# Stick-breaking attention, two heads at a time: values in column halves, products on POOL, copies shared

## Chip, core and metric

The kernel runs on one core of one Trainium2 chip. The metric is the device time of one execution in microseconds (us). Its engines are PE (matmul; PEld is its weight load), ACT, DVE and POOL; SP issues the DMAs. PSUM has 8 banks of 512 fp32 columns on 128 partitions.

## What is computed

A decoder layer on 1024 tokens of width 1024: SwiGLU, a mixer, cross attention into 256 memory tokens, SwiGLU, norm. The change lies in the mixer's stick-breaking attention, 8 heads of 64:

```python
z = jnp.einsum("bhqd,bhkd->bhqk", q_blk, k_pre) * scale      # 128 queries, keys up to them
strict = k_pos[None, :] < q_pos[:, None]
log_rest = jnp.where(strict, jax.nn.log_sigmoid(-z), 0.0)
suffix = lax.cumsum(log_rest, axis=3, reverse=True) - log_rest
a = jnp.where(strict, jnp.exp(jax.nn.log_sigmoid(z) + suffix), 0.0)
outs.append(jnp.einsum("bhqk,bhkd->bhqd", a, v_pre))
```

A weight is thus sigmoid(z) of its key times the product of sigmoid(-z) over all later keys.

## The kernel before

All engines run programs written out by hand, in order, with semaphores. Most of the span is three-pass matmuls of split operands (`three`, L917 to L919). The stick-breaking stage is one loop over `M` = 64 tiles; tile m is head m//8 and a block i of 128 queries, against 128(i+1) keys, so its rows are 128 to 1024 wide. `PAIR_ORDER` takes the blocks of a head as 0,1, 6,7, 2,3, 4,5. At step s:

- PE (L1240): `scores(s)` (L1203 low keys, L1206 the mask on the diagonal, L1208 high keys) into banks 0 to 3; `turn(s-3)` transposes the weights of tile s-3 in blocks of 128 (L1219), four to a bank, through banks 4 to 6; every second step `values` of a pair of query blocks (L1234), 2b+2 fp32 matmuls for pair b. Its stationary operand is the values of two heads (128 columns); of the 128 result rows only the 64 of the head in hand are used. Results go to one half of bank 7.
- ACT (L1647): two sigmoids of the scores, of -z into `rest` (L1654, a ring of 3) and of z into `beta` (L1659, a ring of 4); the copies of the transposed blocks from PSUM into `aT` (by `copy`, L1362); and the rounded high part `act_hi` of the values' result, in the step in which PE makes it.
- DVE (L2197): `stick(s-1)`: a scan of `rest` from the last key to the first (L2190; its second data operand is ignored and is `rest` again), then the product of `beta` and the scanned `rest` one key later, in `beta` (L2194); and the low part `act_lo` of the values' result (by `lo`, L1783).
- SP: `stack_load(h)` brings queries and keys of a head, split in high and low parts, from HBM into one of two slots, six DMAs a head.
- POOL has nothing in this stage.

What ties the steps: the first sigmoid of s waits for the product of s-3; the second for the transposes of s-4; the transposes of m for the product of m and for a free bank; scores of s for a free bank; a scan for its first sigmoid, a product for scan and second sigmoid. Ahead of the loop stand the pool branch's last units (`pool_among`), behind it the output projection `out0`, whose first matmul is the L917 that reads `wb_lo`.

Of the kernel before, what the change touches and what calls it, by code (L numbers as in the profile page):

```python
# [24 lines left out]
P = 128  # L25
# [6 lines left out]
def layer_program(nc, x, mem, ffn1_norm, ffn1_w_gate, ffn1_w_up, ffn1_w_down, mix_norm, w_in, w_pool,  # L32
# [21 lines left out]
    AT_BLOCKS = 12  # L54
    AT_FIRST = {0: 8, 3: 0, 1: 8, 2: 0}
# [3 lines left out]
    with ctx:  # L59
# [112 lines left out]
        sb("arena", [P, ARENA * 256])  # L172
        wa_hi, wa_lo, wa_raw = r1["wa_hi"], r1["wa_lo"], r1["wa_raw"]
        wb_hi, wb_lo, wb_raw = r1["wb_hi"], r1["wb_lo"], r1["wb_raw"]
        q_stack, k_hi2, k_lo2 = r1["q_stack"], r1["k_hi2"], r1["k_lo2"]
# [227 lines left out]
        s_stack = [sem("s_stack0"), sem("s_stack1")]  # L403
# [3 lines left out]
        s_aT_ps, s_aT = sem("s_aT_ps"), sem("s_aT")  # L407
# [167 lines left out]
        W = M // 2  # L575

        turns_before = [0]
        for m in range(M):
            i = 2 * PAIR_ORDER[m % TC // 2] + m % 2
            turns_before.append(turns_before[-1] + i // 4 + 1)  # L580

        def tile_at(m):

            return m // TC, 2 * PAIR_ORDER[m % TC // 2] + m % 2

        def pair_at(w):

            return w // (TC // 2), PAIR_ORDER[w % (TC // 2)]


# [9 lines left out]

        def turns(m):

            i = tile_at(m)[1]
            return [(turns_before[m] + n, 4 + (turns_before[m] + n) % 3, 4 * n, min(4 * n + 4, i + 1))
                    for n in range(i // 4 + 1)]

        def aT_part(buf, m, lo_, hi_):

            first = AT_FIRST[tile_at(m)[1] // 2]
            return buf[:, first + lo_:first + hi_, (m % 2) * P:(m % 2 + 1) * P]  # L610
        STICK_LAG, TURN_LAG, VALUE_LAG = 1, 3, 6
# [21 lines left out]
        def _(sp):  # L633
# [96 lines left out]
            def stack_load(h):  # L730

                if h < 2:
                    sp.wait_ge(a_out, a_done[h - 2])
                else:
                    sp.wait_ge(s_z, TC * (h - 1))
# [3 lines left out]
                rows = slice(64 * h, 64 * (h + 1))  # L739
                for to, lower, upper in ((q_stack, q_spill_hi, q_spill_lo), (k_hi2, k_spill_hi, k_spill_hi),  # L740
                                         (k_lo2, k_spill_lo, k_spill_lo)):
                    sp.dma_start(plain(to[0:64, h % 2]), lower[rows, :]).then_inc(s_stack[h % 2], 16)
                    sp.dma_start(plain(to[64:P, h % 2]), upper[rows, :]).then_inc(s_stack[h % 2], 16)
# [31 lines left out]
            sp.wait_ge(s_z, M)  # L775
# [130 lines left out]


# [6 lines left out]
        def _(pe):  # L914
# [276 lines left out]
            def scores(m):  # L1191
# [3 lines left out]
                if m % TC == 0:  # L1195
                    pe.wait_ge(s_stack[h % 2], 96 * (h // 2 + 1))
# [3 lines left out]
                for lo in range(0, n, HALF):  # L1200
                    keys = slice(lo, min(n, lo + HALF))
                    z = ps[:, z_bank[m][0] + lo // HALF, 0:keys.stop - lo]
                    pe.matmul(z, q_stack[:, h % 2, i * P:(i + 1) * P], k_lo2[:, h % 2, keys],  # L1203
                              start=True, stop=False)
# [3 lines left out]
                    mm = pe.matmul(z, q_stack[:, h % 2, i * P:(i + 1) * P], k_hi2[:, h % 2, keys],  # L1208
                                   start=False, stop=True)
# [13 lines left out]
            def values(w):  # L1223

                h, b = pair_at(w)
# [14 lines left out]
            for s in range(M + VALUE_LAG):  # L1240
# [9 lines left out]
                if s >= VALUE_LAG and (s - VALUE_LAG) % 2 == 0:  # L1250
                    values((s - VALUE_LAG) // 2)
# [1096 lines left out]
```

## Time and profile before

| | us |
|---|---|
| median of 3 runs | 2082.38 (2079.94 to 2085.8) |
| profiled execution | 2080.96 |
| its span, first to last instruction | 2079.2 |
| PE busy | 2001.2 (96%) |
| DVE busy | 1369.4 (66%) |
| ACT busy | 884.9 (43%) |
| POOL busy | 499.6 (24%) |
| granted clock of PE over the span | 0.99 of full speed |

Busy time counts overlapping records once, so it is less than the sum of their durations; a matmul record is longer than the pace at which such records follow each other. A mean stands over all shapes of a line unless the row names one. "Idle before" is an engine's idle time ahead of such an instruction, and what ended it.

### The profile page before, as it was taken

The numbers are of one execution on the slowest core, as the hardware profiler recorded it, in microseconds if no ns is written. First come the engines' busy times: TensorE is split into PE (matmuls) and PEld (weight loads), VectorE is DVE, ScalarE is ACT, GpSimd is POOL, SyncE is SP. The second block draws the span as 40 slices with busy tenths as digits, with TensorE's granted clock in tenths as the row PEclk, the third lists the DMA queues.
The fourth block names the chain that finished last, engine by engine and source line by source line (L and its number), as shares of the span: only waits on it lengthen the run. The fifth ranks groups of instructions, "written<-read, shape, count | busy, mean of one in ns | idle before, by whom it ended". The sixth has DMA issues, their size and how long they took to land. (4 is left out here: it accounts for less than half of the span.)

```text
span 2079.2 us, 25150 instructions
## 1 busy us (share of the span) xinstructions
PE 2001.2 (96%) x9345; PEld 1665.9 (80%) x9345; DVE 1369.4 (66%) x1861; ACT 884.9 (43%) x1571; POOL 499.6 (24%) x360
## 2 busy tenths in 40 slices
PE   6999999999999899898899999999999999999997
PEld 5788888887887688787778888887788888878886
DVE  6765565569798532589745565557755655669896
ACT  6433434434445211477634344443434333334443
POOL 1354555430002121000021100121544554510000
PEclk8999999999999999899999999999999999999999
DMA  4223222254400231343234422231232222265102
GB/s 142 81 71 92 81 76 87 86 195 160 146 21 1 86 102 61 102 91 77 54 94 131 132 82 61 62 111 31 84 89 87 82 78 84 77 238 178 61 1 81
DMA packets 216465, 190.14 MB, mean 91 GB/s; under 512 B 7532, under 2 KB 171928, under 8 KB 216344
## 3 DMA queue, kind: packets, MB, share of 16 engines
q1 hardware_dynamic: 216256, 188.51, 29.4%
q8 instruction: 75, 1.23, 0.3%
q14 instruction: 46, 0.38, 0.1%
q10 hardware_dynamic: 88, 0.02, 0.0%
HBM read 152.85 MB, written 35.65 MB: 91 GB/s over the span
## 5 line engine op out<-in xcount | busy, mean ns | idle before, releaser
L1783 DVE TENSOR_TENSOR w_lo<-st,w_hi 128x512 fp32r<-128x512 f32 x160 | 173.2, 1083 | 178.6 <-ACT w_hi L1362 178.5
L917 PE MATMUL ps<-T_hi,w_lo 128*128 128x512 f32 x640 | 249.3, 390 | 0.3 <-issue 0.3
L918 PE MATMUL ps<-T_lo,w_hi 128*128 128x512 f32 x640 | 249.1, 389 | 0.0
L919 PE MATMUL ps<-T_hi,w_hi 128*128 128x512 f32 x640 | 249.1, 389 | 0.0
L917 PE MATMUL ps<-tr_hi,sr_lo 128*128 128x512 f32 x616 | 242.0, 393 | 5.0 <-DVE xT L2014 2.7
L918 PE MATMUL ps<-tr_lo,sr_hi 128*128 128x512 f32 x616 | 240.0, 390 | 0.0
L919 PE MATMUL ps<-tr_hi,sr_hi 128*128 128x512 f32 x616 | 239.9, 389 | 0.0
L917 PE MATMUL ps<-B_hi,w_lo 128*128 128x512 f32 x576 | 227.0, 394 | 10.8 <-DVE B_lo L1783 4.5
L919 PE MATMUL ps<-B_hi,w_hi 128*128 128x512 f32 x576 | 225.9, 392 | 0.0
L918 PE MATMUL ps<-B_lo,w_hi 128*128 128x512 f32 x576 | 225.7, 392 | 0.0
L871 POOL TENSOR_TENSOR ssq<-sq 128x512 f32<-128x512 f32 x6 | 9.5, 1585 | 612.1 <-issue 425.6
L917 PE MATMUL ps<-act_hi,wb_lo 128*128 128x512 f32 x384 | 153.1, 399 | 3.4 <-DVE wb_lo L1783 1.9
L918 PE MATMUL ps<-act_lo,wb_hi 128*128 128x512 f32 x384 | 150.6, 392 | 0.0
L919 PE MATMUL ps<-act_hi,wb_hi 128*128 128x512 f32 x384 | 150.3, 391 | 0.0
L917 PEld LDWEIGHTS ps<-tr_hi,sr_lo 128*128 128x128 f32 x616 | 115.7, 188 | 33.8 <-DVE tr_lo L1783 9.7
L917 PEld LDWEIGHTS ps<-T_hi,w_lo 128*128 128x128 f32 x640 | 120.2, 188 | 26.0 <-issue 1.1
L918 PEld LDWEIGHTS ps<-T_lo,w_hi 128*128 128x128 f32 x640 | 120.2, 188 | 24.9
L919 PEld LDWEIGHTS ps<-T_hi,w_hi 128*128 128x128 f32 x640 | 120.2, 188 | 24.8
L917 PEld LDWEIGHTS ps<-B_hi,w_lo 128*128 128x128 f32 x576 | 109.2, 190 | 35.5 <-issue 12.9
L1362 ACT ACTIVATE sr_hi<-piece_A 128x512 fp32r<-128x512 f32 x110 | 69.5, 631 | 158.1 <-PE ps L919 141.0
L919 PEld LDWEIGHTS ps<-tr_hi,sr_hi 128*128 128x128 f32 x616 | 115.7, 188 | 24.2
L918 PEld LDWEIGHTS ps<-tr_lo,sr_hi 128*128 128x128 f32 x616 | 115.7, 188 | 23.7 <-issue 0.2
(252 smaller groups left out, 4359.6 us busy)
## 6 DMA issues: line engine op xcount, KB each, us to landing
gate_raw<-in_ffn_w_gate SPq DMA_DIRECT2D x44, 512.0 KB, 5.4
up_raw<-in_ffn_w_up SPq DMA_DIRECT2D x44, 512.0 KB, 5.2
h_spill<-up_s SPq DMA_DIRECT2D x66, 256.0 KB, 2.0
piece_A<-in_ffn_w_down SPq DMA_DIRECT2D x32, 512.0 KB, 4.6
piece_B<-h_spill SPq DMA_DIRECT2D x32, 512.0 KB, 6.0
wa_raw<-in_w_in SPq DMA_DIRECT2D x16, 512.0 KB, 3.9
wb_raw<-in_w_out SPq DMA_DIRECT2D x16, 512.0 KB, 3.9
wb_raw<-in_mem_w_kv SPq DMA_DIRECT2D x16, 512.0 KB, 3.8
```

The source lines that it names most:

```text
L871: pool.tensor_tensor(total, sq[:, 0], sq[:, 1], ALU.add).then_inc(s_ssq, 2)
L917: pe.matmul(to, w_lo, m_hi, start=first, stop=False, skip_group_check=joins)
L918: pe.matmul(to, w_hi, m_lo, start=False, stop=False, skip_group_check=joins)
L919: return pe.matmul(to, w_hi, m_hi, start=False, stop=last, skip_group_check=joins)
L1362: return act.activation(to, src, ACT.Copy, scale=scale)
L1783: return dve.tensor_tensor(to, value, plain(hi), ALU.subtract)
```

## The change

- Order and slots. Two heads go together: groups of four tiles are blocks (0,1), (6,7), (2,3) or (4,5) of one head, then of the other. There are two slots of stacks for two heads each (`q_stack[slot][:, g]`), so `stack_load` waits only from head 4 on, and PE waits for head 1's stack at tile 2.
- Values. `values(w)` serves two heads: for each key block two matmuls with 64 columns of values as stationary operand, head g's into PSUM partitions 64g to 64g+63. There are 160 such matmuls, as before, but all result rows are used. `aT` has 24 blocks for 12. Values run 8 steps behind instead of 6; the high and low parts 9, over 128 partitions, 16 times instead of 32.
- Scan. Its ignored operand is one column of a PSUM bank that nobody writes in the stage (`STILL_BANK`), read with stride 0. The transposes have the other two of banks 4 to 6.
- Products go from DVE to POOL, one per tile as before.
- Copies into `aT`: for blocks 4 to 7 the first four of a tile's blocks (512 columns) are copied by DVE, one step behind its scan; the rest stays with ACT.
- SP waits for 16 tiles fewer before it loads the first output weights.

```diff
-    AT_BLOCKS = 12
-    AT_FIRST = {0: 8, 3: 0, 1: 8, 2: 0}
+    AT_BLOCKS = 24
+    AT_FIRST = {0: 16, 3: 0, 1: 16, 2: 0}
...
-        W = M // 2
+        W = M // 4
+
+        def tile_at(m):
+
+            return 2 * (m // (2 * TC)) + m // 2 % 2, 2 * PAIR_ORDER[m // 4 % (TC // 2)] + m % 2
+
+        def group_at(w):
+
+            return w // (TC // 2), PAIR_ORDER[w % (TC // 2)]
...
+        STILL_BANK = a_bank[A_PROJ + 4]
+        TURN_BANKS = [b for b in (4, 5, 6) if b != STILL_BANK]
+        assert STILL_BANK != 7
+
         def turns(m):
-
             i = tile_at(m)[1]
-            return [(turns_before[m] + n, 4 + (turns_before[m] + n) % 3, 4 * n, min(4 * n + 4, i + 1))
+            return [(turns_before[m] + n, TURN_BANKS[(turns_before[m] + n) % 2], 4 * n, min(4 * n + 4, i + 1))
                     for n in range(i // 4 + 1)]

+        turn_of = [(m, first) for m in range(M) for _, _, first, _ in turns(m)]
+
+        def by_dve(m, first):
+
+            return tile_at(m)[1] >= 4 and first == 0
...
-        STICK_LAG, TURN_LAG, VALUE_LAG = 1, 3, 6
+
+        STICK_LAG, TURN_LAG, VALUE_LAG, OUT_LAG = 1, 3, 8, 9
...
                 if h < 2:
                     sp.wait_ge(a_out, a_done[h - 2])
-                else:
-                    sp.wait_ge(s_z, TC * (h - 1))
+                elif h >= 4:
+                    sp.wait_ge(s_z, 2 * TC * (h // 2 - 1))
...
-            sp.wait_ge(s_z, M)
+            sp.wait_ge(s_z, M - 2 * TC)
...
+            for m in range(M):
+                n = (tile_at(m)[1] + 1) * P
+                pool.wait_ge(s_sig, 2 * (m + 1))
+                pool.wait_ge(s_scan, m + 1)
+                pool.tensor_tensor(beta[:, m % 4, 0:n - 1], beta[:, m % 4, 0:n - 1], rest[:, m % 3, 1:n],
+                                   ALU.mult).then_inc(s_a, 1)
...
-                if m % TC == 0:
-                    pe.wait_ge(s_stack[h % 2], 96 * (h // 2 + 1))
+                slot, g = h // 2 % 2, h % 2
+                if m % (2 * TC) in (0, 2):
+                    pe.wait_ge(s_stack[slot][g], 96 * (h // 4 + 1))
...
-                    if nth >= 3:
-                        pe.wait_ge(s_aT, nth - 2)
+                    if nth >= 2:
+                        pe.wait_ge(*turned(nth - 2))
...
-                pe.wait_ge(s_aT, turns_before[2 * w + 2])
+                hp, b = group_at(w)
+                pe.wait_ge(s_aT, 4 * w + 4)
+                if b >= 2:
+                    pe.wait_ge(s_aT_dve, long_tiles(4 * w + 3))
                 if w:
                     pe.wait_ge(s_o_free, w)
-                pair = slice((h // 2) * P, (h // 2 + 1) * P)
-                o = ps[:, 7, (w % 2) * 2 * P:(w % 2 + 1) * 2 * P]
-                for j in range(2 * b + 2):
-                    lo = P if j == 2 * b + 1 else 0
-                    block = AT_FIRST[b] + j
-                    mm = pe.matmul(o[:, lo:], v_all[:, j, pair], aT[:, block, lo:], start=j == 0, stop=j == 2 * b + 1)
+                n = 2 * b + 2
+                for j in range(n):
+                    lo = P if j == n - 1 else 0
+                    for g in range(2):
+                        o = ps[64 * g:64 * (g + 1), 7, (w % 2) * 2 * P:(w % 2 + 1) * 2 * P]
+                        mm = pe.matmul(o[:, lo:], v_all[:, j, hp * P + 64 * g:hp * P + 64 * (g + 1)],
+                                       aT[:, AT_FIRST[b] + g * n + j, lo:], start=j == 0, stop=j == n - 1)
...
+                        if by_dve(m, first):
+                            continue
                         act.wait_ge(s_aT_ps, nth + 1)
-                        if m % 2 == 0 and first == 0 and m >= 4:
-                            act.wait_ge(s_o, m // 2 - 1)
+                        if m >= 8:
+                            act.wait_ge(s_o, m // 4 - 1)
...
-                dve.tensor_tensor_scan(r[:, ::-1], r[:, ::-1], r[:, ::-1], 1.0, ALU.mult,
-                                       ALU.bypass).then_inc(s_scan, 1)
-                dve.wait_ge(s_scan, m + 1)
-                dve.wait_ge(s_sig, 2 * (m + 1))
-                dve.tensor_tensor(beta[:, m % 4, 0:n - 1], beta[:, m % 4, 0:n - 1],
-                                  rest[:, m % 3, 1:n], ALU.mult).then_inc(s_a, 1)
-
-            for s in range(M + VALUE_LAG):
+                dve.tensor_tensor_scan(r[:, ::-1], r[:, ::-1], ps[:, STILL_BANK, 0:1].broadcast_to([P, n]), 1.0,
+                                       ALU.mult, ALU.bypass).then_inc(s_scan, 1)
...
+                if 0 <= m < M:
+                    for nth, bank, first, end in turns(m):
+                        if not by_dve(m, first):
+                            continue
+                        dve.wait_ge(s_aT_ps, nth + 1)
+                        if m >= 8:
+                            dve.wait_ge(s_o, m // 4 - 1)
+                        dve.tensor_copy(aT_part(aT, m, first, end),
+                                        ps[:, bank, 0:(end - first) * P].rearrange("p (j t) -> p j t", t=P)
+                                        ).then_inc(s_aT_dve, 1)
```

DVE's queue from the low part of one group to the next, before (`rest<-rest` is the scan, `beta<-beta,rest` the product):

```order
L1783 TENSOR_TENSOR act_lo<-ps,act_hi 64x256 [waits s_o_hi]
L2190 SCALAR_TENSOR_TENSOR rest<-rest 128x640 [waits s_sig]
L2194 TENSOR_TENSOR beta<-beta,rest 128x639 [waits s_sig,s_scan]
L2190 SCALAR_TENSOR_TENSOR rest<-rest 128x768 [waits s_sig]
L2194 TENSOR_TENSOR beta<-beta,rest 128x767 [waits s_sig,s_scan]
L1783 TENSOR_TENSOR act_lo<-ps,act_hi 64x256 [waits s_o_hi]
```

and with the change, around the group of blocks 6 and 7 of the second pair of heads:

```order
L1813 TENSOR_TENSOR act_lo<-ps,act_hi 128x256 [waits s_o_hi]
L2220 SCALAR_TENSOR_TENSOR rest<-rest,ps 128x1024 [waits s_sig]
L2220 SCALAR_TENSOR_TENSOR rest<-rest,ps 128x896 [waits s_sig]
L2240 COPY aT<-ps 128x4x128 [waits s_o,s_aT_ps]
L2220 SCALAR_TENSOR_TENSOR rest<-rest,ps 128x1024 [waits s_sig]
L2240 COPY aT<-ps 128x4x128 [waits s_o,s_aT_ps]
L2220 SCALAR_TENSOR_TENSOR rest<-rest,ps 128x384 [waits s_sig]
L2240 COPY aT<-ps 128x4x128 [waits s_o,s_aT_ps]
L1813 TENSOR_TENSOR act_lo<-ps,act_hi 128x256 [waits s_o_hi]
```

The products are gone, the copies (`aT<-ps`) stand between scans, each behind the scan of the tile two after it, and there is one low part for four scans.

PE's queue around the values of blocks 6 and 7, before:

```order
L1203 MATMUL ps<-k_lo,q_stack 128x128 [waits s_sig,s_stack0]
L1206 MATMUL ps<-neg,ident_r 128x128
L1208 MATMUL ps<-k_hi,q_stack 128x128
L1219 MATMUL ps<-ident,beta 128x128 [waits s_aT,s_a]
L1219 MATMUL ps<-ident,beta 128x128 x3
L1234 MATMUL ps<-aT,v_all 128x256 [waits s_o_free,s_aT]
L1234 MATMUL ps<-aT,v_all 128x256 x6
L1234 MATMUL ps<-aT,v_all 128x128
L1203 MATMUL ps<-k_lo,q_stack 128x256 [waits s_sig]
L1206 MATMUL ps<-neg,ident_r 128x128
```

and with the change:

```order
L1231 MATMUL ps<-k_lo,q_stack 128x512 [waits s_sig]
L1235 MATMUL ps<-k_hi,q_stack 128x512
L1231 MATMUL ps<-k_lo,q_stack 128x128
L1233 MATMUL ps<-neg,ident_r 128x128
L1235 MATMUL ps<-k_hi,q_stack 128x128
L1245 MATMUL ps<-ident,beta 128x128 [waits s_aT,s_a]
L1245 MATMUL ps<-ident,beta 128x128 x3
L1262 MATMUL ps<-aT,v_all 64x256 [waits s_o_free,s_aT_dve,s_aT]
L1262 MATMUL ps<-aT,v_all 64x256 x13
L1262 MATMUL ps<-aT,v_all 64x128 x2
L1231 MATMUL ps<-k_lo,q_stack 128x512 [waits s_sig]
```

The 8 matmuls of one head are 16 of 64 columns of two, the transposes in front wait for the product of a tile (`s_a`), and where the last copy but one was DVE's, for `s_aT_dve`.

## Rows read from the trace of the kernel before

**Rows 1.** Windows: start:end, length, busy us (x records) by engine, PE clock, DMA share, GB/s.

```profile
914.98:934.54 19.56, 17.22 (x109) 15.48 (x107) 17.89 (x21) 14.97 (x32) 0.00 (x0) 1.00 0.35 81
sum 39.13, PE 34.99 PEld 31.46 DVE 35.95 ACT 30.58 POOL 0.00; mean PE 17.50 PEld 15.73 DVE 17.97 ACT 15.29 POOL 0.00
```

**Rows 2.** Groups by line, stage (870 to 1036 us): busy us, mean ns, idle before.

```profile
L2190 DVE TENSOR_TENSOR_SCAN rest<-rest 128x128 f32<-128x128 f32 (+3 forms) x64 | 86.3, 1349 | 1.2 <-ACT rest L1654 0.8
L1234 PE MATMUL ps<-aT,v_all 128*128 128x256 f32 (+1 forms) x320 | 68.5, 361 | 1.0 <-DVE act_lo L1783 1.0
L2194 DVE TENSOR_TENSOR beta<-beta,rest 128x127 f32<-128x127 f32 (+3 forms) x64 | 48.5, 758 | 2.2
L1783 DVE TENSOR_TENSOR act_lo<-ps,act_hi 64x256 fp32r<-64x256 f32 x32 | 13.4, 420 | 12.2 <-ACT act_hi L1362 11.7
```

**Rows 3.** Waits in the stage: who for whom, us in total, times, longest.

```profile
ACT act_hi L1362 <- PE ps L1234: 21.1, 11, 2.6
PE ps L1219 <- DVE beta L2194: 17.2, 17, 1.6
```

**Rows 4.** Groups by line and shape, POOL, whole span.

```profile
L844 POOL TENSOR_TENSOR gate_s<-gate_s 128x512 f32<-128x512 f32 x20 | 34.7, 1737 | 0.0
L836 POOL TENSOR_TENSOR up_s<-up_s 128x512 f32<-128x512 f32 x20 | 25.9, 1295 | 37.5 <-ACT up_s L1362 37.5
L897 POOL TENSOR_TENSOR s<-s 128x1024 f32<-128x1024 f32 x6 | 14.4, 2407 | 0.5
```

**Rows 5.** Timeline in the first FFN: start, length, engine, line, instruction.

```profile
95.17 1.40 DVE L1783 TENSOR_TENSOR w_lo<-up_raw,w_hi 128x512 fp32r<-128x512 f32 x1
95.97 1.76 POOL L844 TENSOR_TENSOR gate_s<-gate_s 128x512 f32<-128x512 f32 x1
96.65 0.69 DVE L1932 TENSOR_TENSOR gate_s<-ps,gate_s 128x512 f32<-128x512 f32 x1
...
105.95 0.69 DVE L1783 TENSOR_TENSOR w_lo<-st,w_hi 128x512 fp32r<-128x512 f32 x1 [0.99 <-ACT w_hi L1362]
```

**Rows 6.** Groups by line and shape: DVE's copy out of PSUM.

```profile
L2134 DVE COPY u<-ps 128x512 f32<-128x512 f32 x8 | 5.5, 692 | 25.8 <-PE ps L919 25.8
```

**Rows 7.** Edges of the stage: timeline, key loads' landing, and a window.

```profile
864.84 0.60 SPq L743 DMA_DIRECT2D k_lo<-k_spill_lo  x1
871.13 0.39 PE L1203 MATMUL ps<-k_lo,q_stack 128*128 128x512 f32 x1
...
1034.35 0.48 PE L917 MATMUL ps<-act_hi,wb_lo 128*128 128x512 f32 x1
DMA to landing us min/median/max: 3.4/4.8/6.3
870.00:885.00 15.00, 11.20 (x49) 9.42 (x48) 13.14 (x15) 12.62 (x24) 0.00 (x0) 0.74 0.01 2
```

**Rows 8.** Timeline of one head: scans, scores to transposes, sigmoids, values.

```profile
918.05 2.28 DVE L2190 TENSOR_TENSOR_SCAN rest<-rest 128x1024 f32<-128x1024 f32 x1
...
923.12 0.19 PEld L1203 LDWEIGHTS ps<-k_lo,q_stack 128*128 128x128 f32 x1
...
923.94 0.35 PEld L1219 LDWEIGHTS ps<-ident,beta 128*128 128x128 f32 x3
...
924.24 0.81 ACT L1654 ACTIVATE rest<-ps 128x768 f32<-128x768 f32 x1
...
926.08 3.48 PE L1234 MATMUL ps<-aT,v_all 128*128 128x256 f32 x16
...
928.11 1.75 DVE L2190 TENSOR_TENSOR_SCAN rest<-rest 128x768 f32<-128x768 f32 x1
...
933.29 0.19 PEld L1203 LDWEIGHTS ps<-k_lo,q_stack 128*128 128x128 f32 x1
...
934.23 0.14 PEld L1219 LDWEIGHTS ps<-ident,beta 128*128 128x128 f32 x1
...
934.64 1.02 ACT L1654 ACTIVATE rest<-ps 128x1024 f32<-128x1024 f32 x1 [0.47 <-PE ps L1208]
```

More of the change, by code:

```diff
@@ L402, in layer_program @@
         s_spill = [sem("s_spill0"), sem("s_spill1")]
-        s_stack = [sem("s_stack0"), sem("s_stack1")]
+        s_stack = [[sem(f"s_stack{n}{g}") for g in range(2)] for n in range(2)]
         s_z, s_sig, s_scan = sem("s_z"), sem("s_sig"), sem("s_scan")
@@ L599, in layer_program, with long_tiles, turned @@
         assert all(end <= 4 for _, end in z_bank)
+        def long_tiles(m):
+            return sum(tile_at(k)[1] >= 4 for k in range(m + 1))
+        STILL_BANK = a_bank[A_PROJ + 4]
+        TURN_BANKS = [b for b in (4, 5, 6) if b != STILL_BANK]
+        assert STILL_BANK != 7
         def turns(m):
             i = tile_at(m)[1]
-            return [(turns_before[m] + n, 4 + (turns_before[m] + n) % 3, 4 * n, min(4 * n + 4, i + 1))
+            return [(turns_before[m] + n, TURN_BANKS[(turns_before[m] + n) % 2], 4 * n, min(4 * n + 4, i + 1))
                     for n in range(i // 4 + 1)]
+        turn_of = [(m, first) for m in range(M) for _, _, first, _ in turns(m)]
+        def by_dve(m, first):
+            return tile_at(m)[1] >= 4 and first == 0
+        def turned(nth):
+            m, first = turn_of[nth]
+            return (s_aT_dve, long_tiles(m)) if by_dve(m, first) else (s_aT, m + 1)
         def aT_part(buf, m, lo_, hi_):
-            first = AT_FIRST[tile_at(m)[1] // 2]
+            h, i = tile_at(m)
+            first = AT_FIRST[i // 2] + h % 2 * (i // 2 * 2 + 2)
             return buf[:, first + lo_:first + hi_, (m % 2) * P:(m % 2 + 1) * P]
-        STICK_LAG, TURN_LAG, VALUE_LAG = 1, 3, 6
+        STICK_LAG, TURN_LAG, VALUE_LAG, OUT_LAG = 1, 3, 8, 9
         def next_splits(m, p):
@@ L1239, in _ @@
             pe.wait_ge(s_ident_r, 1)
-            for s in range(M + VALUE_LAG):
+            for s in range(M + OUT_LAG):
                 if s < M:
@@ L1249, in _ @@
                     turn(s - TURN_LAG)
-                if s >= VALUE_LAG and (s - VALUE_LAG) % 2 == 0:
-                    values((s - VALUE_LAG) // 2)
-            pe.wait_ge(s_aT, turns_before[M])
-            pe.wait_ge(s_o_free, W - 2)
+                if VALUE_LAG <= s < M + VALUE_LAG and (s - VALUE_LAG) % 4 == 0:
+                    values((s - VALUE_LAG) // 4)
+            pe.wait_ge(s_aT, M)
+            pe.wait_ge(s_aT_dve, long_tiles(M - 1))
+            pe.wait_ge(s_o_free, W - 4)
             for step in B_STEPS:
@@ L1289, in _ @@
                         ends = d == order[0], d == order[-1]
-                        if n == 0 and d == DC // 2 - 1:
-                            pe.wait_ge(s_o_free, W)
+                        if n < 2 and d == DC // 2 - 1:
+                            pe.wait_ge(s_o_free, W - 1 + n)
                         if kind == "mk":
@@ L1644, in b_weight @@
                 copy(wb_hi[:, n % 2], wb_raw[:, n % 2]).then_inc(b_hi, 1)
-            for s in range(M + VALUE_LAG):
+            for s in range(M + OUT_LAG):
                 if s < M:
@@ L1668, in _ @@
                     for nth, bank, first, end in turns(m):
+                        if by_dve(m, first):
+                            continue
                         act.wait_ge(s_aT_ps, nth + 1)
-                        if m % 2 == 0 and first == 0 and m >= 4:
-                            act.wait_ge(s_o, m // 2 - 1)
+                        if m >= 8:
+                            act.wait_ge(s_o, m // 4 - 1)
                         copy(aT_part(aT, m, first, end),
-                             ps[:, bank, 0:(end - first) * P].rearrange("p (j t) -> p j t", t=P)
-                             ).then_inc(s_aT, 1)
-                if s >= VALUE_LAG and (s - VALUE_LAG) % 2 == 0:
-                    w = (s - VALUE_LAG) // 2
-                    h, b = pair_at(w)
-                    rows = slice(64 * (h % 2), 64 * (h % 2 + 1))
+                             ps[:, bank, 0:(end - first) * P].rearrange("p (j t) -> p j t", t=P)).then_inc(s_aT, 1)
+                if s >= OUT_LAG and (s - OUT_LAG) % 4 == 0:
+                    w = (s - OUT_LAG) // 4
+                    hp, b = group_at(w)
                     act.wait_ge(s_o, w + 1)
-                    copy(a_hi_t[b // 2][rows, h // 2, b % 2 * 2 * P:(b % 2 + 1) * 2 * P],
-                         ps[rows, 7, (w % 2) * 2 * P:(w % 2 + 1) * 2 * P]).then_inc(s_o_hi, 1)
+                    copy(a_hi_t[b // 2][:, hp, b % 2 * 2 * P:(b % 2 + 1) * 2 * P],
+                         ps[:, 7, (w % 2) * 2 * P:(w % 2 + 1) * 2 * P]).then_inc(s_o_hi, 1)
                 if s == M + 2:
```

42 lines of the change are left out of this document (19 added, 23 removed).

## Prediction

> **What bounds the kernel now.** I read the page first: PE is busy 96% of the span, and the chain it follows back runs over PE's projection and FFN lines. That chain breaks off behind the stick-breaking stage, so the stage has to be read by itself. The windows between like points of the work, the 896-wide scans at 895.41, 914.98 and 934.54 [rows 1], give the period of one head, 19.56 us, and of two, 39.13 us. In them DVE is busy 35.95 us, PE 34.99, ACT 30.58 and POOL 0. The reader should see three engines within a fifth of each other: DVE is the fullest, and PE stands right behind it. Eight heads of this (156.5 us) and 6.5 us of edges make the 163 us from the third tile's scores (871.13) to the first output projection (1034.35) [rows 7].
>
> What fills DVE is in the groups of the whole stage [rows 2]: 64 scans for 86.3 us, 64 weighing products for 48.5, 32 low parts for 13.4. PE's values are 320 records, 68.5 us or 8.5 us a head; each matmul of fp32 is two of them, each a pass over the columns. The waits agree: PE waits 17.2 us for DVE's products [rows 3]; ACT (21.1 us [rows 3]) and after it DVE (11.7 us [rows 2]) wait for the value matmuls, since the high part is taken in the same step. So taking work from DVE alone would be stopped after 1 us a pair by PE; both have to shrink.
>
> **The sum, for one pair of heads (39.13 us now; there are four).**
>
> DVE. Removed: products, 48.5/4 = 12.1 us, and half of the low parts, 13.4/8 = 1.7 (16 of 128x256 for 32 of 64x256; the number of columns sets the price, 0.42 us [rows 2]). Added: 8 PSUM copies of 128x512 at 0.69 [rows 6], 5.5 us. 35.95 - 12.1 - 1.7 + 5.5 = 27.7 us. The scan's second operand moves to PSUM: no row has a scan like that. A 128x512 product takes 0.69 us with a PSUM operand and with none [rows 5], so I take 0; bounds are 0 and 0.07 us each (0.69 for the copy [rows 6] against the low part's 0.42 for half the width), 1.1 us a pair.
>
> POOL. 16 products. Its 128x512 operations take 1.29 us alone and 1.74 beside a busy DVE, the 1024-wide one 2.41 [rows 4], where DVE needs 0.69 [rows 5] and about 1.23 (its mean is 0.758 at 575 columns, so a column more costs 1.06 ns); so 1.9 times 12.1 = 23 us, at worst 2.5 times = 31. It was idle before. Its cover is DVE: 23 is below 27.7.
>
> ACT. Removed: 8 copies of 512 columns at 0.52 (half the 1024-wide sigmoid's 1.02 [rows 8]), and half the high parts at the low part's price: 30.58 - 4.2 - 1.7 = about 25 us.
>
> PE. The number of value passes is the same (64 columns out where there were 128, two heads where there was one). Only if the two column halves run at the same time do they cost half: 17.1 becomes 8.5 us, PE 34.99 - 8.5 = 26.5. Each group of values also changes the array's shape and back, 8 changes a pair. Bounds: 0, and 0.36 us each, which is a weight load of 0.19 that is not hidden and some 0.15 us by which a lone record outlasts its pace (3.48 us for 16 value records is 0.22 a record [rows 8], and their mean length is 0.36 [rows 2]). I take 0.2, 1.6 us a pair: PE 28 us.
>
> So the engines need 28, 28, 25 and 23 us, none rules, and what is late next is the **loop** between them: the transposes of tile s-3 wait for its product, scores of s+1 stand behind them on PE, and behind a group's values where there are any. From that product to the product of s+1, four tiles on, it goes: transposes, values, scores of s+1, the 0.4 us until ACT starts, first sigmoid, scan, POOL's product, 0.15 for three handovers. A pair of heads is four groups of four tiles (tile i is 128(i+1) wide), and at the first tile of each group PE does the values of the group two before. By the rows [rows 8]: transposes 0.11 us each (three in 0.35), values 0.22 a record, scores 0.82 for 768 columns (923.12 to 923.94) and 0.94 for 1024 (933.29 to 934.23), sigmoids 0.81 and 1.02, scans 1.75 and 2.28, POOL at 1.9 times the product.
> - Group of tiles 4 and 5 (values of 6 and 7): 0.44 + 3.48 + 0.82 + 0.4 + 0.81 + 1.75 + 1.8 + 0.15 = 9.7 us.
> - Group of 6 and 7 (values of 4 and 5): 0.22 + 2.6 + 0.94 + 0.4 + 1.02 + 2.28 + 2.3 + 0.15 = 9.9.
> - Group of 0 and 1 (values of 2 and 3): 0.66 + 1.7 + 0.4 + 0.15, and for scores to product some 2.2 (a third of the width of the 5.2 us above, with its fixed part): 5.1.
> - Group of 2 and 3 (values of 0 and 1): 0.88 + 0.85 + 0.4 + 0.15 and less than 5.2: under 7.5.
>
> DVE's own work per group is its scans (one tile late; widths between by the line through the two scans), three copies or one (three tiles late) and a low part: 1.22 + 1.48 + 1.75 + 1.48 + 0.69 + 0.42 = 7.0 us for 4 and 5; 8.1 for 6 and 7, 5.7 for 0 and 1, 7.9 for 2 and 3. A group takes the longer: 9.7 + 9.9 + 5.7 + 7.9 = 33.2, and 0.3 for shape changes that lie in a loop: **33.5 us a pair**, 5.6 less than now. Times four: 22.5 us.
>
> Edges. The first tiles go through one engine more, and head 1's stack is needed at tile 2, not 8: its last load is issued at 864.84 and is not needed in the old kernel before 885; PE stands at tile 2 at 871.1 [rows 7], 6 us after the issue, and a load takes 4.8 us in the middle, 6.3 at most [rows 7], so 0 to 1 us. The second pair's twelve loads follow at once; nothing waits for them for 30 us. Filling costs POOL's 2.4 against DVE's 1.2 us on the long tile. The end gets shorter by a value group that is done earlier, about 1 us. I take 2 us in all, bounds 0 and 5. Behind the stage everything is PE's projections and moves as a block.
>
> 2080.96 (the profiled execution; span 2079.2) - 22.5 + 2 = **2060 us**. The median of the runs shown is 2082.38, 0.07% above it, less than their spread, so I keep the number.
>
> **A rule against the trace.** PE's sixteen value records keep a pace of 0.22 us with a weight load each, the loads hidden [rows 8]; all records are 128*128, so no row has a change of shape. The Trainium skill, TensorEngine Tiling (Array Packing), Key Properties, says that changing the tiling mode, not just the tile, drains the engine. If each drain cost the upper bound instead of 0.2 the result would be 2063 (0.16 x 8 x 4 = 5 us on PE, some 3 of it in a loop).
>
> **Rivals.**
> 1. **The halves overlap in part.** For: two passes of one fp32 matmul must follow each other, and the next head's first pass can only join in the middle; against: in a steady run one pass of each head can always go together. If two passes take 1.25 of one, values cost 25% more: 0.87 + 0.65 us in the two loops, 6 us in all: 2066. The Trainium skill, TensorE: Matmul & The Clock Gate, Part 3, gives 2.38 for three column tiles, that is 79% of full overlap.
> 2. **The halves do not overlap (slower).** Then the loops grow by their values: 13.2 + 12.5 + 6.8 + 7.9 + 0.3 = 40.7 us a pair, 1.5 more than now; 6 us in all and 2 of edges: 2089. It decides from the point where a 16-pass group of two heads takes over about 6.5 us instead of 3.5. For: no row shows column halves at all, and PE is already 35 of 39 us. Against: the halves use different columns and PSUM partitions. If the loops smooth out, PE's 36.6 us give 2073.
> 3. **POOL and DVE disturb each other.** For: DVE's products of two SBUF tensors take 1.40 us beside POOL and 0.69 alone [rows 5], and POOL's 1.76 for 1.29. Against: the one with an operand in PSUM took 0.69 in the middle of a POOL operation of 1.76 [rows 5], and every DVE operation of the new stage has at most one SBUF input. If the scan counts as two all the same, scans and products queue: 21.6 + 23 + 5.5 + 1.7 = 51.8 us a pair, +51: 2133.
> 4. **The loops are looser than I think**, and DVE's 28.7 us (the groups' sum) and 1 for handovers rule: 4 x 9.4 less, 2 more: 2045.
> 5. **PE's clock.** PE's busy share falls from 89% to 80%. In the first 15 us of the stage, with PE busy for 11.2 of them, the granted clock was 0.74 [rows 7], a mix of 1.2 and 2.4 GHz; after that it was 1.00 [rows 1]. At 0.74 throughout, 28 us of PE become 38: 2078.
>
> **Chances.** Forecast (2052 to 2068) 0.50; partial overlap 0.15; no overlap 0.17; disturbance 0.06; DVE alone 0.08; clock 0.04. A measurement of this kernel can tell 0.3%, 6 us, from no change. Faster by more: forecast, partial overlap, DVE alone and a tenth of no overlap (its smooth end, 2073), 0.75. Within it: the clock and a quarter of no overlap, 0.08. Slower: the disturbance and the rest of no overlap, 0.17. The range leaves out the disturbance, most of DVE alone and the upper end of no overlap, some 0.2 together: 2048 to 2084, the edges' bounds and the scan's 1.1 us a pair included.
>
> **What would show it.** In the profile after: (a) a two-head group of tiles 6,7 (32 records) in about 3.5 to 4 us from its first to its last value matmul; 7 means rival 2. (b) Scans of 2.28 us at 1024 wide, POOL products near 2.3; scans over 2.5 mean rival 3. (c) From one 896-wide scan to the same one a pair later 33.5 us, with DVE busy some 28. (d) The waits: no ACT wait of 21 us for value matmuls, in its place PE's transposes waiting for POOL, and DVE's scans for ACT's sigmoids. (e) First output projection at about 1014 instead of 1034.35; the rest of the span, 1044.9 us, unchanged. If the period is above 37 us I am wrong on the overlap or the loop; below 31, on the loop.

## Result and profile after

The changed kernel takes 2086.17 us (median of 20 runs, 2082.61 to 2091.94), the kernel before 2081.61 (20 runs, 2078.72 to 2085.8). The ratio is 1.002 (95% interval 1.0014 to 1.0027): slower by 0.2%, where 1% faster was forecast. The profiled execution took 2084.46 us with a span of 2082.6. The stage is read in the same views as before, the windows of a pair of heads first, as in [rows 1]. The 896-wide scans at 913.44, 954.65 and 995.87 enclose two pairs of heads:

```profile
913.44:954.65 41.21, 32.83 (x220) 24.87 (x217) 26.86 (x28) 25.48 (x53) 19.07 (x16) 0.92 0.33 76
954.65:995.87 41.22, 32.87 (x220) 24.61 (x217) 26.86 (x28) 25.52 (x53) 19.06 (x16) 0.92 0.13 33
```

A pair takes 41.2 us instead of 39.13, though the three engines that were busy before have less to do: DVE 26.86 us, ACT 25.48, PE 32.83. POOL's 19.07 are new. No engine is busy for 80% of the time. PE's clock, 1.00 before, is 0.92. Now the groups of the stage by line (busy us, mean ns, idle before), against [rows 2]:

```profile
L2220 DVE TENSOR_TENSOR_SCAN rest<-rest,ps 128x128 f32<-128x128 f32 (+3 forms) x64 | 84.5, 1342 | 7.4 <-ACT rest L1684 7.4
L2240 DVE COPY aT<-ps 128x512 f32<-128x512 f32 x32 | 21.5, 673 | 14.7 <-PE ps L1245 14.7
L1813 DVE TENSOR_TENSOR act_lo<-ps,act_hi 128x256 fp32r<-128x256 f32 x16 | 6.8, 425 | 31.7 <-ACT act_hi L1392 31.7
...
L931 POOL TENSOR_TENSOR beta<-beta,rest 128x127 f32<-128x127 f32 (+3 forms) x64 | 76.3, 1202 | 161.0 <-DVE rest L2220 158.3 <-ACT beta L1689 2.6
...
L1262 PE MATMUL ps<-aT,v_all 128*64 128x256 f32 (+1 forms) x320 | 41.7, 417 | 0.6 <-ACT aT L1392 0.6
```

The scans cost what they did, the values 41.7 us for 68.5. What has grown is the idle time behind the bar of a small group: 6.8 us of low parts have 31.7 us of it, where it was 12.2. The waits of the stage:

```profile
ACT rest L1684 <- PE ps L1235: 39.5, 22, 3.5
DVE act_lo L1813 <- ACT act_hi L1392: 31.7, 11, 4.8
PE ps L1245 <- DVE aT L2240: 23.0, 19, 2.3
PEld ps L1245 <- POOL beta L931: 17.7, 10, 2.6
...
DVE rest L2220 <- ACT rest L1684: 7.4, 9, 1.5
```

The timeline shows what such a wait for the high part holds up. This is the group of tiles 4 and 5, with the values of 6 and 7 at its head:

```profile
933.92 3.46 PE L1262 MATMUL ps<-aT,v_all 128*64 128x256 f32 x32
...
934.30 1.49 DVE L2220 TENSOR_TENSOR_SCAN rest<-rest,ps 128x640 f32<-128x640 f32 x1 [0.22 <-ACT rest L1684]
...
937.31 0.50 PE L1231 MATMUL ps<-k_lo,q_stack 128*128 128x512 f32 x1
...
938.44 0.81 ACT L1684 ACTIVATE rest<-ps 128x768 f32<-128x768 f32 x1 [3.08 <-PE ps L1235]
...
939.14 0.81 ACT L1689 ACTIVATE beta<-ps 128x768 f32<-128x768 f32 x1
...
939.83 0.50 ACT L1392 ACTIVATE aT<-ps 128x384 f32<-128x384 f32 x1
...
940.20 0.41 ACT L1392 ACTIVATE act_hi<-ps 128x256 fp32r<-128x256 f32 x1
...
940.64 0.42 DVE L1813 TENSOR_TENSOR act_lo<-ps,act_hi 128x256 fp32r<-128x256 f32 x1 [4.85 <-ACT act_hi L1392]
...
940.98 1.74 DVE L2220 TENSOR_TENSOR_SCAN rest<-rest,ps 128x768 f32<-128x768 f32 x1
```

The values are done at 937.4. Their high part stands in ACT's queue at the end of the step: behind two sigmoids and a copy, of which the first waits for scores that PE makes after the values. It starts at 940.20. DVE's low part waits for it, and in DVE's queue it stands **ahead of the next scan**. The scan had its sigmoid at 939.25 (938.44 + 0.81) and starts at 940.98, 1.73 us later. The scan is in the loop, the low part is not.

**Theory 1**, drawn from these rows: the low part's place behind a late high part stops the scans; either end of that chain can be moved to repair it. **Theory 2**: the transposes have two banks instead of three, DVE's copies out of them stand behind scans (PE waits 23.0 us for them), and taking products and copies to other engines is what made the loop long. Two rivals come from the prediction: the column halves gain less than they seem to, or the scan's PSUM operand costs something.

### The profile page after: what moved, and what is told of

It is laid out like the page before. It is cut to its first block and busy times, and to the rows that moved or that the text cites. A ratio compares the mean times of both kernels' runs of the same rounds, so it can differ in the third digit from the quotient of the medians.

```text
span 2082.6 us, 25157 instructions
## 1 busy us (share of the span) xinstructions
PE 1991.9 (96%) x9345; PEld 1639.2 (79%) x9345; DVE 1334.0 (64%) x1813; ACT 863.9 (41%) x1523; POOL 575.9 (28%) x424
## 5 line engine op out<-in xcount | busy, mean ns | idle before, releaser
L944 PEld LDWEIGHTS ps<-tr_lo,sr_hi 128*128 128x128 f32 x616 | 115.8, 188 | 23.7 <-issue 0.2
L1392 ACT ACTIVATE w_hi<-st 128x512 fp32r<-128x512 f32 x160 | 99.9, 626 | 80.5 <-PE ps L945 63.1
```

What stands on the lines that cost most here:

```text
L944: pe.matmul(to, w_hi, m_lo, start=False, stop=False, skip_group_check=joins)
L1392: return act.activation(to, src, ACT.Copy, scale=scale)
```

## Experiments

Each experiment was run beside the kernel before on the same chip; that kernel's medians stand between 2081.2 and 2082.9 us, and each ratio is against them. The changed kernel was not run again beside them: differences against its 2086.17 us, and between experiments of different chips, carry some 2 us of doubt.

### The low part one step later

```diff
-                if s >= OUT_LAG and (s - OUT_LAG) % 4 == 0:
-                    w = (s - OUT_LAG) // 4
+                if s >= OUT_LAG + 1 and (s - OUT_LAG - 1) % 4 == 0:
+                    w = (s - OUT_LAG - 1) // 4
```

In DVE's loop, which runs one step longer.

> DVE takes the low part of a value group one step later, behind the next scan instead of ahead of it; nothing else moves. Theory 1 (the low part holds up DVE's queue: it waits for ACT's high part, which stands behind two sigmoids and a copy, and the next scan, whose sigmoid is long done, stands behind it): in one pair of heads of the changed kernel the scan behind a low part starts 1.73, 0.87, 1.73 and 0.35 us after its sigmoid and DVE's own work would let it, 4.7 us in all; period 41.2 down to about 36.5 us, time 2086 - 19 = 2067 (2062 to 2074). Theory 2 (the loop over PE's value matmuls, scores, sigmoid, scan and product sets the period, and the low part only waits in time that is lost anyway): within 3 us of the changed kernel, 2083 to 2088.

2062.5 us, ratio 0.990 (0.9885 to 0.9919): 23.7 us less than the changed kernel, and 34.67 us a pair. That is at the lower end of what theory 1 allowed, and 1.8 us a pair below its 36.5. The one wait was worth more than the 22 us that the whole change was forecast to gain.

### The high part ahead of the sigmoids of its step

In ACT's loop, the lines that make `act_hi` stand at the step's start instead of its end:

```diff
             for s in range(M + OUT_LAG):
+                if s >= OUT_LAG and (s - OUT_LAG) % 4 == 0:
...
+                    act.wait_ge(s_o, w + 1)
+                    copy(a_hi_t[b // 2][:, hp, b % 2 * 2 * P:(b % 2 + 1) * 2 * P],
+                         ps[:, 7, (w % 2) * 2 * P:(w % 2 + 1) * 2 * P]).then_inc(s_o_hi, 1)
                 if s < M:
```

> ACT takes the high part of a value group ahead of the two sigmoids and the copy of its step; DVE's order stays. Theory 1: the high part is done about 0.5 us after the value matmuls, the low part no longer waits, the same 4.7 us a pair go: 2067 (2062 to 2074), like the late low part. Theory 2: no change, 2083 to 2088. A third way: ACT now waits for the value matmuls ahead of a sigmoid whose scores were ready before; that would make it slower than the late low part by up to 1 us a group, 2067 to 2083.

2059.1 us, ratio 0.9887 (0.987 to 0.9903), 27.1 us less than the changed kernel, and below the 2062 to 2074 expected: 6.8 us a pair went, not 4.7. A window of a pair, and the timeline at the place shown above:

```profile
910.18:944.58 34.40, 29.88 (x220) 22.73 (x217) 26.92 (x28) 25.80 (x53) 19.08 (x16) 1.00 0.40 91
```

```profile
927.17 3.46 PE L1262 MATMUL ps<-aT,v_all 128*64 128x256 f32 x32
...
930.68 0.39 ACT L1392 ACTIVATE act_hi<-ps 128x256 fp32r<-128x256 f32 x1 [2.07 <-PE ps L1262]
931.10 0.42 DVE L1813 TENSOR_TENSOR act_lo<-ps,act_hi 128x256 fp32r<-128x256 f32 x1 [2.06 <-ACT act_hi L1392]
...
932.53 1.75 DVE L2220 TENSOR_TENSOR_SCAN rest<-rest,ps 128x768 f32<-128x768 f32 x1 [1.01 <-ACT rest L1690]
```

Both parts are done before the sigmoid is, and the scan now waits for the sigmoid, as the prediction's loop has it. ACT even waits 17.5 us in the stage for values, ahead of sigmoids, and loses nothing: their scores come later still. Where the 6.8 us a pair went shows when the scan of each group's second tile starts, counted from the pair's 896-wide scan in either kernel:

| scan of | changed kernel | high part first | difference | more than in the row above |
|---|---|---|---|---|
| tile 7, 1024 wide | 5.80 | 4.09 | 1.71 | 1.71 |
| tile 3, 512 wide | 16.88 | 13.39 | 3.49 | 1.78 |
| tile 5, 768 wide | 27.54 | 22.35 | 5.19 | 1.70 |
| tile 1, 256 wide | 37.58 | 30.78 | 6.80 | 1.61 |

Two of the four steps, 1.71 and 1.70, are the stopped scan itself: in both places it starts 1.73 us after its sigmoid's end in the changed kernel, and 0.03 or 0.04 us after it with the high part first. Of tile 3's 1.78 another 0.75, and of tile 1's 1.61 another 0.09, lie between the sigmoid's end and the scan. The other 2.55 us stand ahead of these two sigmoids, in stretches in which PE's clock fell in the changed kernel. Ahead of these stretches PE waits for DVE's copy (2.33 and 1.87 us), which stands behind two late scans:

```profile
924.15 1.06 PE L1245 MATMUL ps<-ident,beta 128*128 128x128 f32 x8 [2.33 <-DVE aT L2240]
```

The granted clock ahead of the first such stretch, in it, and in the second one:

```profile
918.00:924.00 6.00, 2.76 (x15) 2.06 (x15) 5.11 (x5) 5.23 (x10) 2.34 (x2) 1.00 0.00 0
924.00:930.00 6.00, 5.85 (x33) 4.67 (x34) 4.35 (x6) 3.12 (x8) 4.20 (x3) 0.72 0.01 3
945.00:951.00 6.00, 5.52 (x35) 3.93 (x35) 3.26 (x5) 1.83 (x7) 2.59 (x3) 0.72 1.02 231
```

PE was busy for 2.76 of the six microseconds before the clock fell; 0.72 is a mix of 1.2 and 2.4 GHz. The same 220 records keep PE busy for 32.83 us in the changed kernel and 29.88 here, at a clock of 1.00; these 2.95 us are of the size of the 2.55. DMA traffic doesn't tell the two kernels apart: its share was 0.01 in the first stretch and 1.02 in the second, and with the high part first it reached 1.02 between 936 and 942 us at a clock of 1.00. That the clock causes the 2.55 us was not tried by itself. Both repairs bring it back to 1.00, so I count it as a part of the price of the wait.

### Both repairs at once

> Both repairs together: the high part ahead of ACT's sigmoids and the low part one step later in DVE's queue. With the high part first alone (2059.1 us) DVE still waits 8.8 us for high parts over the stage. If what is lost is what DVE waits for, this gives 2052 to 2056. If the loop over scores, sigmoids, scan, product and transposes sets the period (34.40 us a pair with DVE busy some 27), the wait is time that DVE has to spare and the time stays within 3 us of 2059; the low part one step later can then even cost 1 to 3 us by freeing the value bank later.

2061.6 us, ratio 0.9899 (0.9884 to 0.9914), 34.63 us a pair. The repairs do not add up: they open the same chain at two ends. What DVE still waited for the high part was time it had to spare; the expected gain to 2052 to 2056 did not come. Of the 2.5 us more than with the high part first alone, 0.9 are in the four periods. The rest shows at the edges in the profiled executions (the output projection starts at 1016.04 for 1013.26), but the two ratios' intervals overlap.

### Column halves head after head

```diff
-                for j in range(n):
-                    lo = P if j == n - 1 else 0
-                    for g in range(2):
+                for g in range(2):
+                    for j in range(n):
+                        lo = P if j == n - 1 else 0
```

The same matmuls on the same columns, but all of one head's first. On the changed kernel:

> The value matmuls of a group go head after head instead of taking turns, so that two passes in a row are always in the same column half; same instructions, same number. If the column halves run at the same time because they take turns: a group of tiles 6 and 7 takes 6.9 us instead of 3.4, 8.5 us of PE more in a pair of heads, of which the three groups whose values stand in the loop pay all: 6 to 8.5 us a pair, 2110 to 2120. If the overlap does not depend on the order, or the 3.4 us have another reason: no change.

2103.1 us, ratio 1.0097 (1.0082 to 1.0112): 16.9 us more than the changed kernel, or 4 to 5.3 a pair, where 6 to 8.5 were expected. And on the one with the high part first, where it is the prediction's rival 2 without the stopped scan:

> High part first, and the values head after head, so that the column halves do not run at the same time: rival 2 of the prediction in a kernel whose queue order does not stop it. By the loop sum the values of a group count twice, 40.7 us a pair less some 0.9 for one or two changes of shape saved and the 34.40 against 33.5 measured: 40.5 to 41.6, 2083 to 2089. If PE's busy time sets it instead (28 to 30 us a pair and 8.5 more), 36.5 to 38.5: 2068 to 2076. If taking turns matters little here: within 3 us of 2059.

2081.8 us, ratio 0.9998 (0.9989 to 1.0008), 22.7 us more than with turns. A window of a pair, and one group of 32 records, PE:

```profile
914.52:954.25 39.73, 35.24 (x218) 26.32 (x216) 26.92 (x28) 25.81 (x53) 19.10 (x16) 1.00 0.36 83
```

```profile
933.29 6.10 PE L1262 MATMUL ps<-aT,v_all 128*64 128x256 f32 x32
```

6.10 us instead of 3.46: nearly all that the halves give, they give only when the two heads take turns (twice the 3.48 us of 16 records of the full width would be 6.96). The expectations had 6.9 us for such a group and 40.5 to 41.6 us a pair. The period is 1 us under the 40.7 of rival 2 and well above PE's 35.2 us busy: the loop sum holds here too, the sum of busy times doesn't.

### The scan's ignored operand back in SBUF

```diff
-  dve.tensor_tensor_scan(r[:, ::-1], r[:, ::-1], ps[:, STILL_BANK, 0:1].broadcast_to([P, n]), 1.0,
+  dve.tensor_tensor_scan(r[:, ::-1], r[:, ::-1], r[:, ::-1], 1.0,
```

> The scan's ignored operand is the SBUF tile again, as before the change, with the products still on POOL. If two SBUF inputs on DVE and POOL's products disturb each other: scans beside a product grow from 2.28 to over 3 us at 1024 wide and products from 1.9 to over 2.5; 19 us of products a pair lie beside scans, DVE has 14 us idle a pair, so 5 to 19 us a pair, 2106 to 2160. If the scan does not read its second operand when it is ignored: no change, scans of 2.28 us and 2086.

2099.7 us, ratio 1.0081 (1.0066 to 1.0096), 13.5 more than the changed kernel, or 2.6 to 3.4 a pair; 5 to 19 a pair were expected. Groups of the stage:

```profile
L2220 DVE TENSOR_TENSOR_SCAN rest<-rest 128x128 f32<-128x128 f32 (+3 forms) x64 | 106.1, 1683 | 6.0 <-ACT rest L1684 6.0
...
L931 POOL TENSOR_TENSOR beta<-beta,rest 128x127 f32<-128x127 f32 (+7 forms) x63 | 111.6, 1792 | 140.3 <-DVE rest L2220 140.3
```

The scan takes 1683 ns for 1342 and POOL's product 1792 for 1202. With POOL idle the same scan took 1349 ns in the kernel before [rows 2]. So an operand that the scan ignores slows both engines when it lies in SBUF and they work side by side, and costs nothing in PSUM. The Trainium skill, GPSIMD Engine Reference, Specifications, says that POOL contends with DVE instructions that have two SBUF inputs. This trace agrees, also for an input that isn't used.

### Copies on ACT, products on DVE

With the high part first, all copies of transposed weights go to ACT, and the waits count ACT's copies:

```diff
         def by_dve(m, first):
-            return tile_at(m)[1] >= 4 and first == 0
+            return False
```

In a second kernel the products also go back to DVE, behind their scans, and POOL rests.

> High part first, and all PSUM copies of the transposed weights on ACT again, none on DVE. Theory 2 (DVE's copies stand behind its scans, and PE, with two banks to transpose into, waits for them: 10.6 us over the stage with the high part first): PE's wait goes, up to 8 us off, 2050 to 2056. Rival (ACT gets 8 copies of 0.52 us a pair more, 4.2 us, on top of 25.5, and its sigmoids, which start each loop, stand behind them): 2 to 4 us a pair more, 2067 to 2075.

> High part first, copies on ACT, and the weighing products back on DVE behind their scans, POOL idle in the stage: of the change only the two heads at a time and the values in column halves are left. By busy times DVE has 26.9 - 5.5 + 12.1 = 33.5 us a pair. If POOL's weighing is needed, DVE's queue sets the period: 36 to 38 us a pair instead of 34.4, 2065 to 2073. If it buys nothing (the loop gets shorter by the 1.1 us that DVE is faster on a long product), the time is within 3 us of the run with copies on ACT and POOL's products.

2068.5 us (ratio 0.993, 0.9913 to 0.9947) and 2074.3 (0.9957, 0.9943 to 0.9972). Two pairs of each:

```profile
915.47:950.82 35.35, 29.65 (x220) 22.77 (x217) 22.86 (x21) 28.80 (x61) 19.09 (x16) 1.00 0.35 79
950.82:987.79 36.97, 31.26 (x220) 23.44 (x216) 22.85 (x21) 28.79 (x61) 19.07 (x16) 0.95 0.22 53
```

```profile
914.43:952.62 38.19, 31.34 (x220) 23.76 (x217) 34.26 (x37) 29.01 (x61) 0.00 (x0) 0.96 0.41 94
952.62:989.21 36.59, 29.74 (x220) 22.80 (x217) 34.03 (x36) 29.00 (x61) 0.00 (x0) 1.00 0.16 42
```

Theory 2 falls as far as the engines go: with the copies on ACT, PE's matmuls wait 14.0 us for them, where they waited 10.6 for DVE's and 3.1 for ACT's, and the kernel is 9.4 us slower. POOL's weighing is worth 5.9 us more in that kernel. The two parts of the change that I held for a burden both pay. That the transposes have two banks and not three was tried in no run.

### The copies ahead of the scans

With the high part first, DVE's copy of a step is put ahead of its scan: in DVE's loop `stick(s - STICK_LAG)` moves behind the block that begins with `if 0 <= m < M`.

```diff
-                if 0 <= s - STICK_LAG < M:
-                    stick(s - STICK_LAG)
...
                 if 0 <= m < M:
                     for nth, bank, first, end in turns(m):
...
+                if 0 <= s - STICK_LAG < M:
+                    stick(s - STICK_LAG)
```

> High part first, and in DVE's queue each copy of transposed weights ahead of the scan of its step instead of behind it. With the high part first PE waits 10.6 us over the stage for DVE's copies. If these waits lie in the loop, up to 8 us come off the 2059.1: 2051 to 2056. If the copy then holds the scan back (it waits itself for PE's transposes, which wait for POOL's product), DVE's waits move from the low part to the scan and the time rises by 3 to 15 us: 2062 to 2074.

2069.7 us, ratio 0.9934 (0.992 to 0.9948), 10.6 more than with the high part first alone. The waits of the stage name it:

```profile
PEld ps L1245 <- POOL beta L931: 21.0, 27, 1.8
...
PE ps L1245 <- POOL beta L931: 15.2, 17, 1.6
...
DVE aT L2232 <- PE ps L1245: 13.1, 20, 1.1
```

It is the fault of the changed kernel again: what waits (the copy, for transposes, 13.1 us) stands ahead of a scan that could run, and POOL's products, which need the scan, come late for PE (21.0 us in its weight loads, where it was 9.9, and 15.2 in the matmuls that follow these loads; the two overlap).

### The values in two halves

With the high part first, a group's value matmuls are issued in two blocks, behind the transposes of two tiles in turn; `OUT_LAG` is 10.

```diff
-                for j in range(n):
+                for j in range(part * n // 2, (part + 1) * n // 2):
...
-                if VALUE_LAG <= s < M + VALUE_LAG and (s - VALUE_LAG) % 4 == 0:
-                    values((s - VALUE_LAG) // 4)
+                if VALUE_LAG <= s < M + VALUE_LAG and (s - VALUE_LAG) % 4 < 2:
+                    values((s - VALUE_LAG) // 4, (s - VALUE_LAG) % 4)
```

> High part first, and a group's value matmuls in two halves on PE, one behind the transposes of one tile and one behind those of the next, the high and low parts one step later. The loop of the prediction (transposes, values, scores, sigmoid, scan, product) holds all values of a group in its first step: 3.5, 2.6, 1.7 and 0.9 us. If that is what sets the 34.40 us a pair, spreading them over two steps gives each step time in which DVE is behind anyway: 1 to 2 us a pair, 2051 to 2056. If the loop only moves the same time to the next step: within 3 us of 2059. Against it: 8 more changes of the array's shape a pair are not needed (each half is one block), but 8 more entries and exits are, at 0.17 us each 1.4 us a pair, 2062 to 2065 where nothing is won.

2053.7 us, ratio 0.9866 (0.9853 to 0.988): the fastest kernel here, 27.5 us under the one before. A pair and the low parts:

```profile
908.68:941.42 32.74, 30.26 (x220) 22.35 (x217) 26.91 (x28) 25.67 (x53) 19.16 (x16) 1.00 0.42 97
```

```profile
L1815 DVE TENSOR_TENSOR act_lo<-ps,act_hi 128x256 fp32r<-128x256 f32 x16 | 6.5, 408 | 0.3 <-ACT act_hi L1394 0.3
```

The values stood whole in one turn of the loop; spread over two, 1.66 us a pair go. ACT's wait for values falls from 17.5 to 3.4 us in the stage at the same time, and DVE's for the high part from 8.8 to 0.3; by the late low part above, which gained nothing, the second is not what pays. Whether the shorter stretch of values on PE or ACT's shorter wait pays was not separated. PE is now busy for 30.26 of 32.74 us, and near being the bound. With the copies ahead of the scans as well, that cost stays:

> Both together: values in two halves, and DVE's copies ahead of the scans. If each takes its own wait away, the sum of the two gains against 2059.1; if the copy ahead of the scan costs, about the time of that run less what the halves give. The fastest I expect is 2048.

2067.5 us, ratio 0.9929 (0.9916 to 0.9941): 13.8 us more than with the halves alone.

### The low part one step later in the kernel before

High part one step later and ahead of ACT's sigmoids, low part one step later; both loops run a step longer.

```diff
-                if s >= VALUE_LAG and (s - VALUE_LAG) % 2 == 0:
+                if s > VALUE_LAG and (s - VALUE_LAG) % 2 == 1:
```

The diff shows the condition, the same in both loops. On ACT it moves nothing: the high part stood at the end of a step and now stands at the start of the next, ahead of the same sigmoid as before. The timelines of both kernels show the same order on ACT between 914 and 934 us. Only at the end of the stage one high part, and one low part on DVE, change places with two weight blocks of the next stage. So this run tries one thing in the loop, the low part behind one more scan and product in DVE's queue.

> The kernel before, with the value outputs' high part one step later and ahead of ACT's sigmoids, and the low part one step later in DVE's queue. Theory: the wait in ACT's queue for the values of the same step (21.1 us over the stage, and 11.7 on DVE behind it) is the same fault as in the changed kernel; a head then takes DVE's 18.0 us busy and little more, 8 x 1.0 to 1.5 = 8 to 12 us off: 2070 to 2075. Rival: PE's 17.5 us a head, with its waits for DVE's products, holds the period at 19.56 us whatever ACT does: within 3 us of the kernel before.

2091.7 us, ratio 1.0044 (1.0029 to 1.0059): slower, which neither side of the expectation had. Two waits of the stage, the low part ahead of a 16-record group of values, and these values:

```profile
ACT act_hi L1362 <- PE ps L1234: 37.1, 16, 5.2
...
PE ps L1234 <- DVE act_lo L1783: 8.8, 9, 2.9
```

```profile
927.79 0.42 DVE L1783 TENSOR_TENSOR act_lo<-ps,act_hi 64x256 fp32r<-64x256 f32 x1
```

```profile
928.36 5.17 PE L1234 MATMUL ps<-aT,v_all 128*128 128x256 f32 x16 [1.91 <-ACT aT L1362]
```

A group there comes every two steps, not four, and PE's values wait until the low part of the group before them is done (`s_o_free`). Here that is at 928.21 (927.79 + 0.42), and the values start at 928.36. The profile puts the wait down to ACT's copy, which also ends late. During these values, from 928.36 to 933.50, the granted clock is 0.67, and they take 5.17 us instead of 3.48. The head with this stretch (914.41 to 936.33) takes 21.92 us, the next one, at a clock of 1.00 throughout, 19.74, for 19.56 before: most of the price lies in the stretches at the lower clock. The high part, whose place is the old one, waits longer because its values end later (37.1 us for 21.1 [rows 3]).

So there is no rule that a later low part helps. In the changed kernel it had time to spare and stood in the way of a scan; here PE needs it soon. Whether another order gains in the kernel before is open: the high part was not moved there, and letting values wait only for the low part that last used their own half bank was not tried.

## Why the prediction was wrong

**What failed is the loop term**, 33.5 us a pair. It followed one chain, from product to product, and let each instruction start when its inputs were there. It never asked where in DVE's queue the low part stands. The prediction had the clue: ACT's wait for value matmuls and DVE's 11.7 us behind it, "since the high part is taken in the same step", and wrote in (d) that this wait would go. ACT's did; it moved to the first sigmoid (39.5 us for scores), and the high part behind it came later than before, so DVE's grew from 11.7 us to 31.7. The Trainium skill, PSUM — Partial Sum Buffer, Engine vs sequencer instructions, says that the queues of ScalarE, VectorE and GpSimdE are strictly first in, first out. The trace agrees (a scan 1.73 us behind its sigmoid). With the wait out of the queue the period is 34.40 us, and the time 2059.1. The chain itself was right: with the high part first, the four stretches from product to product (the ends of POOL's products of tiles 7, 3, 5, 1 and 7 again) are 7.3, 10.0, 6.4 and 10.7 us, for 7.9, 9.7, 5.7 and 9.9 in the sum.

Point by point, measured against forecast, per pair:
- **DVE** 26.9 us for 27.7; **ACT** 25.5 for 25; the copies 0.673 us for 0.69. All three were sized well.
- **POOL** 19.1 for 23. The 1.9 times DVE's product holds for no width: the mean is 1202 ns for 758, 1.59 times, and the product of 1023 columns 2.00 us for DVE's 1.22. The 128x512 operations that the 1.9 was read from took 1.29 us, the product of 511 columns 1.09; why they differ is open.
- **PE** 29.9 at clock 1.00 for 28; 32.8 in the changed kernel at 0.92.
- **The scan with a PSUM operand (test b)** 0 more, as taken (1342 ns for 1349).
- **Overlap (test a)**: 32 records in 3.46 us, at the lower end of the 3.5 to 4 forecast. Rivals 1 and 2 don't happen; rival 2's period was priced well (39.73 us a pair when forced, for 40.7), its 2089 was 7 us too high.
- **Rival 3** was averted by the PSUM operand, as argued. Forced on the changed kernel, it costs 13.5 us and not 51: the scans grow by a quarter and the products by a half, they don't take turns.
- **Rival 4** did not come: 32.74 us even with the values spread, against 29.7 (28.7 and 1).
- **Rival 5**, the clock at 0.74 throughout, did not come. The period's mean was 0.92, with 0.72 in the stretches that follow PE's long waits.
- **Edges**: 2 us were added. With the high part first the output projection starts at 1013.26, 21.1 us earlier than [rows 7], of which four periods give 18.9: the edges gain 2.2 us. That is 4.2 us better than forecast, and four periods of 34.40 for 33.5 are 3.6 us worse; the two about cancel, so that 2060 meeting 2059.1 is in part luck.
- **Test (c)** said that a period over 37 us means the overlap or the loop. 41.2 us, and the overlap holds: the loop.

The range ended at 2084; the result lies 2 us above it. No rival had a queue in which an instruction with time to spare stops a needed one; the slower ones were about the column halves and about POOL and DVE in each other's way. So 0.5 was far too much for a loop sum that had not been held against the order of the queues. That the result lies near the range is no merit of the sum, whose period was off by 7.7 us a pair.

## What to carry to other kernels

When work is cut and no engine stays full, write each engine's queue down and ask of every instruction that waits what stands behind it and who needs that: an instruction nobody is in a hurry for must stand where its input is already there, or behind the ones the loop needs. A repair is checked in the same way: the low part one step later gave 24 us in the changed kernel and cost 10 in the kernel before. And where busy times have fallen but the period hasn't, look at the small groups with a large idle time before them, not at the big ones.

## What the hardware showed

- Two matmul streams on the two column halves run side by side when their instructions take turns: 32 records in 3.46 us, what 16 records of the full width took before (3.48 [rows 8]); and 6.10 us when one head follows the other. At each change of the array's shape, into the halves and back, PE's weight loads stand idle for 0.17 us, against 0.2 taken and 0.36 as the bound. The Trainium skill, TensorEngine Tiling (Array Packing), Key Properties, says that a change of mode drains the engine. The trace agrees as far as this short gap shows it:

```profile
933.92 3.22 PEld L1262 LDWEIGHTS ps<-aT,v_all 128*64 128x64 f32 x32 [0.17 <-issue]
...
937.31 0.19 PEld L1231 LDWEIGHTS ps<-k_lo,q_stack 128*128 128x128 f32 x1 [0.17 <-issue]
```

- An SBUF operand that an instruction ignores is not free: beside POOL it slowed the scan by 25% and POOL's product by 49%.
- A wait on PE can cost more than its length: behind one of 2.33 us the granted clock was 0.72 for six microseconds, in which PE was busy for 5.85; behind one of 1.91 us in the kernel before with the late low part it was 0.67, and 16 value records took 5.17 us instead of 3.48.
